# Two transformer-style blocks in split float32r: the streamed activation buffers moved within 512 bytes of SBUF

## The reference

```
h    = rmsnorm(x);  proj = h @ w_in                        # 7 kinds of columns, plus gates
y_a  = (bg * conv3(cg * xv)) @ w_a_out
y_b  = gated_delta_rule(q, k, v, a, b), gated by z, @ w_b_out
x    = x + (sig(ga) * y_a + sig(gb) * y_b) @ w_o
x    = x + (silu(gate) * val) @ w_down,  gate, val = split(conv3(rmsnorm(x) @ w_up))
x    = rmsnorm(x)
# second block
proj = rmsnorm(x) @ w_in_2                                 # attention q k v, retention q k v g, gates
o_a  = dilated attention in three groups;  o_r = groupnorm(retention) * silu(gr)
x    = x + (sig(ta) * (o_a @ w_proj_a) + sig(tb) * (o_r @ w_proj_b)) @ w_out
x    = x + relu(rmsnorm(x) @ w_up_2)**2 @ w_down_2
```

## Time and profile before

| | |
|---|---|
| runs, us | 1152.54, 1151.12, 1154.89; median 1152.54 |
| the profiled execution, us | 1156.57 |
| its span (first to last instruction), us | 1154.8 |
| mean granted TensorE clock | 0.995 |
| TensorE matmul busy, us | 1133.9 (98%) |
| weight load busy, us | 1104.9 (96%) |
| VectorE, ScalarE, GpSimd busy, us | 769.7, 603.1, 205.9 |
| bytes read from HBM | 190.27 MB |

### The profile page before, as it was taken

The page is one execution under the profiler, slowest core; times in us unless marked ns, Lnnn a source line. Parts: engine busy times, 40 slices in busy tenths (PEclk is TensorE's granted clock), DMA queues, the critical chain, the costliest instruction groups (busy, mean ns, idle before and its releaser), DMA issues. The chain is left out here.

```text
span 1154.8 us, 23245 instructions
## 1 busy us (share of the span) xinstructions
PE 1133.9 (98%) x10262; PEld 1104.9 (96%) x10262; DVE 769.7 (67%) x875; ACT 603.1 (52%) x692; POOL 205.9 (18%) x129
## 2 busy tenths in 40 slices
PE   9989899999999999999899999999999999999998
PEld 7989889999999999999899999999999999999998
DVE  6999775445456897796779757645666556756453
ACT  6978333242664765565655534433797335544341
POOL 0442364210133200000445400000011002211010
PEclk9999999999999999999999999999999999999999
DMA  8434333234365555555555553445444555555552
GB/s 304 152 137 150 119 111 106 81 111 135 121 224 201 194 185 187 208 191 186 179 178 182 168 187 126 142 146 183 151 144 172 190 184 183 183 188 208 189 188 105
DMA packets 27748, 192.81 MB, mean 167 GB/s; under 512 B 3072, under 2 KB 3200, under 8 KB 4992
## 3 DMA queue, kind: packets, MB, share of 16 engines
q1 hardware_dynamic: 27648, 191.33, 48.5%
HBM read 190.27 MB, written 1.05 MB: 166 GB/s over the span
## 5 line engine op out<-in xcount | busy, mean ns | idle before, releaser
L1236 DVE TENSOR_TENSOR wl<-raw,wh 128x2048 fp32r<-128x2048 f32 (+1 forms) x178 | 421.9, 2372 | 133.3 <-ACT wh L909 132.1
L909 ACT ACTIVATE wh<-raw 128x2048 fp32r<-128x2048 f32 x176 | 336.5, 1913 | 248.0 <-DMA raw<-in_wts 246.8
L566 PE MATMUL psS<-Yh,wh 128*128 128x256 f32 x1056 | 300.6, 285 | 1.5 <-issue 1.0
L566 PE MATMUL psS<-Yh,wl 128*128 128x256 f32 x1056 | 293.6, 278 | 0.0
L566 PE MATMUL psS<-Yl,wh 128*128 128x256 f32 x1056 | 293.5, 278 | 0.0
L566 PE MATMUL psS<-Xh,wh 128*128 128x256 f32 x896 | 260.2, 290 | 7.7 <-issue 6.7
L566 PE MATMUL psS<-Xl,wh 128*128 128x256 f32 x896 | 251.3, 280 | 0.0
L566 PE MATMUL psS<-Xh,wl 128*128 128x256 f32 x896 | 251.2, 280 | 0.0
L566 PEld LDWEIGHTS psS<-Yh,wh 128*128 128x128 f32 x1056 | 199.2, 189 | 4.7 <-issue 3.3
L566 PEld LDWEIGHTS psS<-Yl,wh 128*128 128x128 f32 x1056 | 198.8, 188 | 2.5 <-issue 1.9
L566 PEld LDWEIGHTS psS<-Yh,wl 128*128 128x128 f32 x1056 | 198.5, 188 | 0.0
(11 more groups left out here) (246 smaller groups left out, 2000.4 us busy)
## 6 DMA issues: line engine op xcount, KB each, us to landing
raw<-in_wts SPq DMA_DIRECT2D x176, 1024.0 KB, 4.8
raw<-in_wts SPq DMA_DIRECT2D x2, 512.0 KB, 6.1
gdn<-in_x SPq DMA_DIRECT2D x1, 1024.0 KB, 7.9
out<-head SPq DMA_DIRECT2D x4, 256.0 KB, 2.1
head<-in_x SPq DMA_DIRECT2D x1, 516.0 KB, 4.0
head<-in_x SPq DMA_DIRECT2D x1, 512.0 KB, 6.3
head<-in_sel SPq DMA_DIRECT2D x1, 512.0 KB, 3.9
xf<-in_dr SPq DMA_DIRECT2D x1, 512.0 KB, 5.7
```

The lines of the kernel that those rows point to most:

```text
L566: mm = pe.matmul(bank[:, half], a[:, n % SLOTS, p, :], b[:, kk_, :], start=(first and i == 0), stop=(last and i == 2), skip_group_check=True)
L909: act.activation(wh[:, n % SLOTS], raw[:, n % SLOTS], ACT.Copy).then_inc(sem["wh"], 1)
L1236: return dve.tensor_tensor(out, a, b, op)
```

## The change

Three tensors that nothing uses are allocated, of 192, 64 and 192 bytes per partition. Y moves by 192 bytes, X (and `xf` over it) by 256, and Z, O, `gdn`, `mix2` and all that is allocated behind them by 448. Modulo 512, Y is then at 0, X at 64, Z and O at 256; `wh`, `wl`, `raw` and everything ahead of Y stay where they were. The order of instructions, their shapes and their waits are the same on every engine.

```
@@ -305,9 +305,11 @@
         ss = [sb(f"ss{i}", [P, 2, S]) for i in range(2)]
         small = sb("small", [P, 64])
         rtok = sb("rtok", [P, 2])
+        sb("pad_y", [P, 48])
         Yh, Yl = sb("Yh", [P, KT, S], F32R), sb("Yl", [P, KT, S], F32R)
 
 
+        sb("pad_x", [P, 16])
         with ExitStack() as own:
             Xh, Xl = sb("Xh", [P, KT, S], F32R, own), sb("Xl", [P, KT, S], F32R, own)
         xf = sb("xf", [P, 4096])
@@ -315,6 +317,7 @@
         md = xf[:, 3072:3840].rearrange("p (g i) -> p g i", g=3)
         ST = [xf[:, a:a + 384] for a in (0, 384, 1024, 1408)]
 
+        sb("pad_z", [P, 48])
         with ExitStack() as own:
             ga_ = sb("gdn", [P, 8, KT, S], F32, own)
         with ExitStack() as own:
```

## The result

The changed kernel takes 1173.49 us (median of 4 runs, 1170.08 to 1173.97) against 1152.32 of the kernel before; the ratio is 1.0156, 95% interval 1.0114 to 1.0198. It is slower: by 18 us at that ratio, by 21 between the two medians. The forecast was 1144, and its range ended at 1163.

A forecast was written before the change was run, and what follows sets the result against it. TensorE's matmul line, busy 98% of the span, was taken as the bound. Pads and other engines at 0, long slow stretches -6.5 and a quarter of the rest -2.1 sum to -8.6 us: 1152.5 to 1144 us, range 1137 to 1163.

The forecast's parts named there:

- What bounds the kernel: TensorE's unbroken line of matmuls, busy in 98% of the span; each faster matmul shortens the path by 4.5 ns.
- The pads and the other engines at 0: Unused allocations, and VectorE, ScalarE and GpSimd work on the moved buffers, were each set at a cost of 0.
- That the place matters, and by its distance from the weights: In TensorE's streams, the distance modulo 512 from weight tile to moving row affects the pace, 113.3 or 117.8 ns.
- the hints: Pace changes at the L554/L566 handovers at 791.89 and 677.67 us, and 24 of 24 fast matmuls at L588.
- Which way it goes: TensorE's streams get faster: long slow stretches clear, -6.5 us, and a quarter of the rest, -2.1; sum -8.6 us.
- the hint: At L588, stationary rows of 256 bytes at distance 0 or 256 from X: 24 of 24 fast, median 276 ns.
- The bounds: Limits for TensorE's streams: all slow matmuls turning fast, -14.8 us; all fast ones turning slow, +22 us.
- Rival D: A third, slower pace that the trace doesn't show; at 123 ns throughout, some +67 us, to 1220; chance 0.02.
- Rival A: Nothing to measure: stream restarts set the phase, the address doesn't enter; time stays 1152.5 us; chance 0.22.
- Rival B: Slower: handovers between X, Y and Z shift streams; half the matmuls in fast stretches slow, +7.8 us, 1160; chance 0.28.
- Rival C: A much faster stream, 106.7 ns between matmul starts through placement; -72 us, to 1081; chance 0.03.
- The check by count: Slow distances near 1,300 to 1,400 instead of 3,322 if right; 117.8 ns inside 391 to 571 us, from a handover, if wrong.

The follow-up runs named there:

- w_moved: Changed kernel's places for Y, X, Z and O, with weights wh and wl moved by 64 bytes; 1172.50 us, ratio 1.0169 against the kernel before.
- m1: The matmul stream by itself, other engines idle: stationary tiles at 128, moving rows at 0 to 496 in steps of 16 bytes; 113.3 to 120.0 ns between starts.
- m3: The matmul stream by itself with stationary tiles of 128, 64 and 32 columns at six moving-row places; floor of 113.3 ns at every width.
- x_only: Kernel before with X alone moved, to 64 modulo 512; Y, Z and O stay at 320; 1154.60 us, ratio 1.0014.
- y_only: Kernel before with Y alone moved, to 0 modulo 512; X, Z and O stay at 320; 1166.54 us, ratio 1.0118.
- m4: The matmul stream by itself: stationary tiles at 16, 32 and 48 modulo 256, moving rows at 0 to 240; tiles at 16, distance 192: 113.8 to 114.2 ns.

## Why the prediction was wrong

**What bounds the kernel: right.** The difference of the spans is in the distances between the starts of TensorE's matmuls; waits, clock and the other engines stayed. That each faster matmul shortens the path by its full 4.5 ns holds the other way too: 19.7 us of longer distances gave 17.4 us of span.

**The pads and the other engines at 0: right.** 2376 and 1913 ns for the split, as before.

**That the place matters, and by its distance from the weights: right.** w_moved shows it, with X and Y swapping their paces when the weights alone moved by 64 bytes. It is the distance modulo 256, together with the tile's place modulo 32. But the hints that the prediction took it from did not show it: here it was right by luck. At the handovers of the earlier trace rows the distance changes between 64 and 192 modulo 256, and in m1 each of the two runs at 117.8 in some pieces and at 113.3 in others; such a change of pace needs no change of distance.

**Which way it goes: the step that failed.** The sum took -8.6 us "because the distance under which slow stretches settle is given up everywhere at once, and the nearest row at an even multiple of 128 is fast". Neither half holds. X did not give the distance up: -64 and +192 are the same modulo 256, and X kept its two paces. The others did, and went where it is slower. The row was L588, whose distances of 0 and 256 no stream took: Y is at -128, Z and O at +128, which is one distance modulo 256, and m1 measured 118.5 to 120.0 ns there. Nor would the row have held at its own distance, since its tile has 64 columns: m3 has 113.5 and 113.6 ns there in two pieces of three, and 119.7 to 119.9 with 128 columns. The prediction called the hint weak because the stretch before was fast; the stronger reasons, another shape and another distance, stood in the same row. In place of -8.6 us the term measured +19.7.

**The bounds: too narrow above.** +22 us stood for every matmul at 117.8, worked out from the two paces of the trace. But the kernel before has its streams at the distances 192 and 64 modulo 256, and no row of it could give a price for 128. Rival D came nearest, a third pace with a chance of 0.02, though the 120 ns that it reads in the earlier trace rows are rounding: the trace has 119, 119 and 117 ns for these three, and no twelve distances in a row of L554 and L566 have a mean above 118.3 in that kernel. At 128 lie Y, Z, O and the swapped ones now, 5,212 matmuls with means of 118.7 to 119.2 ns and whole stretches at 120.0. With 120.0 in the bounds the range would have reached to +34: 5,212 matmuls by 6.7 ns, 3,103 of X by 4.5, less the 14.8 us that lay at 117.8 already. 1152.5 + 34 is 1186.5, and 1173 would have been inside.

**Rival A (nothing) is out** for Y, Z and O; for X alone it is right (x_only, 0.9980 to 1.0048). **Rival B (handovers)**, with 0.28, had the sign but not the cause: Y within a run of Y blocks is at 120.0, in y_only as in the changed kernel; and an X block behind a Y block is back at 113.3 after 3 of 47 distances. **Rival C (106.7 ns)**: no place of 16 or 4 bytes went below 113.3.

**The check by count.** Distances of 117.8 ns inside 391 to 571 us, beginning at a handover, were to show rival B. What came was 120.0 from 393 us on, within a run of Y blocks, which no line of the list had.

What stays open is the mechanism behind the table. That both operands have a part is shown: in m1 the place of the moving rows alone changes the pace, in w_moved that of the weights alone. That their two reads get in each other's way is the likely reason, and no run shows it directly. A rule that gives 113.3, 116.7, 118.3 or 120.0 from the two places was not found, only the table.

## What to carry to other kernels

Where TensorE's matmuls follow one another without a gap, the distance between their starts is the thing to read, not their duration, and it can depend on where both operands lie in SBUF. Sweep the places of the streamed row and the stationary tile in steps of 16 bytes with the kernel's own shapes, in a stream by itself, before choosing pads: a row with another tile width says nothing of it. Where a trace shows two paces at one clock, repeat the run, since the split between them may be drawn anew. And where a change brings a distance that the trace doesn't have, its paces don't bound the new one: leave room above them.

## What the runs showed of the hardware that was not expected

- A float32r matmul of 256 columns settles at no mean distance below 113.3 ns at full clock at any place tried, while at half clock it takes 213 ns, twice 106.7. The 6.7 ns are there with tiles of 128, 64 and 32 columns (m3).
- The pace repeats every 256 bytes of the moving row's place (m1) and, but for two distances of 16, every 32 bytes of the tile's (m4); four bytes from a fast place (240) it is already 119.9 and 121.6 ns.
- With the distance at 64 or 192 modulo 256 and the tile on a multiple of 32, a stream runs at either of two paces, and stays there, but for inserted steps, for 225 us in the kernel before (344 to 571 us) and for the last 170 us of x_only's trace, at 113.3 ns in the one and 117.8 in the other. The ten runs of x_only differ by 1.5%, the 12 runs of the kernel shifted by 16 bytes by 0.3%.
